# A hybrid recurrent encoder layer on eight cores: conv buffers on page bounds, more staging slots, pauses that take no turn, and an earlier norm of tile 3

## What is computed

```
h = rmsnorm(x, g_mix)
q, k, v, o, if, f_h, i_h, q_h, g_h, gate_a, gate_b = split(h @ w_in)
q, k = silu(causal_conv4(q, k))                    # width 4, per channel
hm, C, n, m = mlstm_chunkwise(q, k, v, i, f)        # matrix memory, 4 heads
y_a = (rmsnorm(hm) * sigmoid(o)) @ w_branch_a
oh, S = hgrn2_chunkwise(q_h, 1 - f, i_h, log f)     # f = lb + (1-lb)*sigmoid(f_h)
y_b = (rmsnorm(oh) * silu(g_h)) @ w_branch_b
x = x + (sigmoid(gate_a)*y_a + sigmoid(gate_b)*y_b) @ w_out
x = x + square(relu(rmsnorm(x, g_ffn) @ w_ff1)) @ w_ff2
y = rmsnorm(x, g_final)
```

## Time and profile before

| | us |
|---|---|
| timed runs: median (lowest, highest) of 3 | 4442.13 (4436.71, 4608.5) |
| profiled execution, its own time | 4419.51 |
| its span, slowest core (cores 4383.6 to 4418.2) | 4418.2 |
| TensorE busy, of the span | 4057.9 |
| ScalarE, VectorE busy | 1386.1, 1387.1 |

### The profile page before, as it was taken

How to read it: one execution, slowest core, us unless ns; L and a number is a source line. 1 busy time by engine, 2 the same in 40 slices (tenths; PEclk the granted TensorE clock), 3 DMA queues, 4 the chain that set the end, 5 groups by cost and what they waited for, 6 DMA issues and landing times.

```text
span 4418.2 us, 60194 instructions; the slowest of 8 cores (4383.6 to 4418.2 us)
## 1 busy us (share of the span) xinstructions
PE 4057.9 (92%) x22402; PEld 1944.4 (44%) x22402; DVE 1387.1 (31%) x2519; ACT 1386.1 (31%) x2730; POOL 272.8 (6%) x517
## 2 busy tenths in 40 slices
PE   6779878889799999997999999998999999999999
PEld 3334334334344444443444444444444445444444
DVE  4325265222333432224233422222542331310012
ACT  4445355221433332104333321124433311122212
POOL 0000000000000000000000000000000000000000
PEclk9989889999899999998999999999999999999999
DMA  9888867888687878986777789876888897677775
GB/s 180 168 178 164 180 136 146 175 165 156 130 173 140 162 137 192 174 168 125 161 148 140 142 176 192 170 148 126 174 155 166 166 196 131 118 125 130 124 125 120
DMA packets 142711, 682.91 MB, mean 155 GB/s; under 512 B 24496, under 2 KB 54712, under 8 KB 69080
## 3 DMA queue, kind: packets, MB, share of 16 engines
q0 software_dynamic: 73872, 536.94, 69.7%
q1 hardware_dynamic: 53344, 111.78, 7.4%
q10 hardware_dynamic: 15208, 30.35, 2.1%
HBM read 1157.17 MB, written 58.74 MB: 275 GB/s over the span
## 4 chain that ended last, share of the span: by engine, by line
PE 78%; DMA 8%; DVE 5%; ACT 5%; issue 3%; ACTq 0%; DVEq 0%; SPq 0%; POOL 0%; POOLq 0%
PE psb L294 76%; DMA wslot<-wu 3%; ACT rr L263 2%; DMA iS<-aa 2%; PE psb L302 1%; DMA kS<-aa 1%; DVE uh L280 1%; DVE rr L272 1%; ACT rq L263 1%; ACT uh L263 1%; DVE rr L280 1%; DVE rr L276 1%; DMA rr<-xp 1%; ACT aa L263 1%; DMA xt<-xp 1%
## 5 line engine op out<-in xcount | busy, mean ns | idle before, releaser
L294 PE MATMUL psb<-ht,wslot 128*128 128x512 bf16 x4096 | 926.7, 388 | 58.4 <-DMA wslot<-wu 24.3
L294 PE MATMUL psb<-wslot,aa 128*128 128x512 bf16 x4096 | 907.2, 381 | 27.9 <-ACT aa L263 26.6
L294 PE MATMUL psb<-uh,wslot 128*128 128x512 bf16 x4096 | 905.7, 380 | 2.6 <-DVE uh L272 1.9
L294 PEld LDWEIGHTS psb<-ht,wslot 128*128 128x128 bf16 x4096 | 405.1, 100 | 559.5 <-issue 107.3
L294 PEld LDWEIGHTS psb<-wslot,aa 128*128 128x128 bf16 x4096 | 396.5, 98 | 503.8 <-issue 46.4
L294 PEld LDWEIGHTS psb<-uh,wslot 128*128 128x128 bf16 x4096 | 396.2, 98 | 471.0 <-issue 12.3
L104 POOL DMA_DIRECT2D wslot<-wu x512 | 272.1, 536 | 4083.6 <-PE psb L294 3897.9
L272 DVE TENSOR_TENSOR xt<-psb,xt 128x512 f32<-128x512 f32 x320 | 221.1, 691 | 956.9 <-PE psb L294 956.7
L263 ACT ACTIVATE rq<-psb 128x512 f32<-128x512 f32 (+1 forms) x320 | 166.9, 521 | 659.0 <-PE psb L294 642.1
L263 ACT ACTIVATE aa<-psb 128x512 f32<-128x512 f32 x160 | 95.3, 595 | 576.8 <-PE psb L294 537.3
L263 ACT ACTIVATE rr<-rr 128x512 f32<-128x512 f32 (+9 forms) x322 | 169.8, 529 | 241.6 <-DVE rr L272 147.5
(11 more groups left out here) (186 smaller groups left out, 2978.6 us busy)
## 6 DMA issues: line engine op xcount, KB each, us to landing
wslot<-wu POOLq DMA_DIRECT2D x512, 1024.0 KB, 13.7
xt<-xp SPq DMA_DIRECT2D x22, 1024.0 KB, 31.1
yp<-xt SPq DMA_DIRECT2D x12, 1024.0 KB, 12.9
ht<-hS SPq DMA_DIRECT2D x5, 2048.0 KB, 12.9
fS<-aa SPq DMA_DIRECT2D x16, 512.0 KB, 15.8
rr<-fS ACTq DMA_DIRECT2D x16, 512.0 KB, 9.4
rr<-xp SPq DMA_DIRECT2D x6, 1024.0 KB, 20.2
vS<-aa SPq DMA_DIRECT2D x8, 512.0 KB, 16.1
```

Of the source, the lines that this page charges most:

```text
L294: ins = pe_e.matmul(out, lhsT=l, rhs=r, start=(i == 0), stop=(i == n - 1))
```

## The change

Five things:

1. **Conv buffers.** The two pads lie at 0 and 2304, three accumulators at 4608 + 2048k, so that none shares a page with another; the conv counter goes through 2 pads, 3 accumulators and 2 `sg` buffers. The put-off `fin` of a unit's last chain, and the store behind it, now run after the next chain's first reads, in the next unit too.
2. **Staging slots.** Tile 0 has eight (4 in `aa`, 4 in `hg`), tile 1 four, tile 2 eight until its unit 9 (4 in `aa`, 4 in `xt`), then four; the fills of t = 0 and 1 have six (2 in `rr`), that of t = 2 four. The sample frames have four of 512 bytes, of which a V or IH result takes two. The gate results take a slot like the others.
3. **Pauses and turns.** A pause yields "w". `pull` then tries the other lane too, and a turn passes only if both pause. In `p12` a chain of K or Q is worth half a pull, any other chain one and a half; elsewhere one, as before. Two pauses are added in `norm_block` between the scaled row and its transposes, and tile 0's recurrence takes the longer form with pauses (`sp`).
4. **Norm of tile 3.** It has two x buffers in `xt`; the first two loads are issued at unit 11 of `p12` of tile 2. A block's next load is issued right after its scaling.
5. **Place of `norm2`'s buffers**: `hg` at 8192 and 12288 for t < 3.

```diff
@@ pull, tick
-                    next(q[0])
-                    bg["last"] = nm_
-                    return True
+                    r = next(q[0])
                 except StopIteration:
                     q.pop(0)
-        return False
+                    continue
+                if r == "w":
+                    waited = True
+                    break
+                bg["last"] = nm_
+                return True
+        return waited
-    def tick():
-        bg["acc"] += bg["rate"]
+    def tick(w=1.0):
+        bg["acc"] += w
@@ norm_block
         yield
+        yield "w"
+        yield "w"
         for half in range(2):
@@ norm1
-            yield from norm_block(xv[0:LB, :], xv.p(), LB, xnviews[b % len(xnviews)], b, PO_GMIX, dst, t0)
+            g = norm_block(xv[0:LB, :], xv.p(), LB, xnviews[b % len(xnviews)], b, PO_GMIX, dst, t0)
+            yield next(g)
+            if b + n < nb:
+                x_load(T, xviews, b + n)
+            yield from g
...
-            if b + n < nb:
-                load(b + n)
-                if n == 1:
-                    for _ in range(5 if blocks is not None else 3):
-                        yield
+            if b + n < nb and n == 1:
+                for _ in range(3):
+                    yield "w"
@@ p12
+        def stage(kind, nb, dt, *shape):
+            stg[kind] += 1
+            if kind == "p":
+                k = stg["p"] % len(slots)
+                return slots[k][0].v(slots[k][1], dt, *shape), f"stp{k}"
...
-                            cv["i"] ^= 1
+                            cv["i"] += 1
                             ns, sl = (1, 512) if p else (2, 32)
-                            o = cvoff + cv["i"] * 4112
-                            pad, acc = cvbuf.v(o, F32, ns, sl + 3), cvbuf.v(o + 2064, F32, ns, sl)
-                            sg = cvbuf.v(cvoff + 8224, F32, ns, sl) if cv["i"] else rq.buf.v(0, F32, ns, sl)
+                            pad, acc = cvbuf.v((cv["i"] % 2) * 2304, F32, ns, sl + 3), cvbuf.v(4608 + (cv["i"] % 3) * 2048, F32, ns, sl)
+                            sg = sg0[0].v(sg0[1], F32, ns, sl) if cv["i"] % 2 else rq.buf.v(0, F32, ns, sl)
...
-                            if late:
-                                late.pop()()
+                                if store is not None:
+                                    store()
+                            flush()
                             late.append(fin)
                         if p:
-                            tick()
-                    if late:
-                        late.pop()()
+                            tick(1.5 if kind == "QH" else 0.5)
@@ build_program, the calls
-    for t in (1, 2):
+    for t in (0, 1, 2):
         tiles[t]["sp"] = True
-    p12([tiles[0]], 0, 12, b_uh, 0, 3, pre0, at0)
+    p12([tiles[0]], 0, 12, b_uh, sg_e, sl(b_aa, 0, 4) + sl(b_hg, 0, 4), pre0, at0)
-    p12([tiles[1]], 0, 12, b_uh, 0, 3)
+    p12([tiles[1]], 0, 12, b_uh, sg_e, sl(b_aa, 0, 4))
-    p12([tiles[2]], 0, 12, b_uh, 0, 3)
+    x3v = [b_xt.v(16384, F32, 2048), b_xt.v(24576, F32, 2048)]
+    at2 = {11: lambda: [x_load(tiles[3], x3v, b) for b in range(2)]}
+    p12([tiles[2]], 0, 12, b_uh, sg_e, sl(b_aa, 0, 4) + sl(b_xt, 16384, 4), None, at2, 9)
...
-                lanes["a"].append(norm1(tiles[3], [b_rr.v(8192, F32, 2048)], [b_rr.v(16384, BF16, 2048)], bl, 8))
+                lanes["n"].append(norm1(tiles[3], x3v, [b_rr.v(16384, BF16, 2048)], bl, 0, True))
...
-            p12([tiles[3], TS_], fill[t][0], fill[t][1], b_rr, 0, 3)
+            p12([tiles[3], TS_], fill[t][0], fill[t][1], b_rr, (b_rr, 10752), sl(b_aa, 0, 4) + (sl(b_rr, 20480, 2) if t < 2 else []))
```

More of the change, by code:

```diff
@@ L428, in norm_block, with x_load, norm1 @@
         yield
-    def norm1(T, xviews, xnviews, blocks=None, gap=4):
+    def x_load(T, xviews, b):
+        LB = T["LB"] if T["kind"] == "p" else 64
+        src = xp[T["id"] * 512:(T["id"] + 1) * 512, :] if T["kind"] == "p" else xs
+        xv = xviews[b % len(xviews)]
+        S.dma("sp", f"xl{b % len(xviews)}", xv[0:LB, :], src[b * LB:(b + 1) * LB, :], (), xv.p())
+    def norm1(T, xviews, xnviews, blocks=None, gap=4, loaded=False):
         LB = T["LB"] if T["kind"] == "p" else 64
         nb = 4 if T["kind"] == "p" else 1
-        src = xp[T["id"] * 512:(T["id"] + 1) * 512, :] if T["kind"] == "p" else xs
         n = len(xviews)
[L436 to L440, removed]
+        if not loaded:
+            for b in range(min(n, nb)):
+                x_load(T, xviews, b)
         for _ in range(gap):
-            yield
+            yield "w"
         for b in range(nb):
@@ L462, in hload, with p12, flush @@
               sum((DR("H", t, b) for b in range(4)), []), T["hT"].p())
-    def p12(ctxs, lo, hi, cvbuf, cvoff, nst, pre=None, at=None):
-        stg = {"i": 0}
+    def p12(ctxs, lo, hi, cvbuf, sg0, slots, pre=None, at=None, cut=None):
+        stg = {"p": 0, "s": 0}
         cv = {"i": 0}
+        late = []
+        def flush():
+            if late:
+                late.pop()()
+        def stage(kind, nb, dt, *shape):
[3 more added lines that the diff above has]
+                return slots[k][0].v(slots[k][1], dt, *shape), f"stp{k}"
+            if nb > 512:
+                stg["s"] += stg["s"] % 2
+                k = stg["s"] % 4
+                stg["s"] += 1
+            else:
+                k = stg["s"] % 4
+            return hgs.buf.v(k * 512, dt, *shape), f"sts{k}"
         for ui, (kind, u) in enumerate(P12U[lo:hi]):
@@ L469, in p12 @@
                 at[ui]()
+            if cut is not None and ui == cut:
+                slots = slots[:4]
             (wt,) = ws_take([UB[kind] + u])
@@ L1064, in build_program @@
     at0 = {3: lambda: lanes["n"].append(norm1(tiles[1], x0v[0:2], [b_uh.v(12288, BF16, 2048)], None, 10))}
-    p12([tiles[0]], 0, 12, b_uh, 0, 3, pre0, at0)
+    sl = lambda b, lo, n: [(b, lo + 4096 * k) for k in range(n)]
+    sg_e = (hgs.buf, 0)
+    p12([tiles[0]], 0, 12, b_uh, sg_e, sl(b_aa, 0, 4) + sl(b_hg, 0, 4), pre0, at0)
     tiles[0]["rh_ok"] = True
@@ L1087, in hook @@
         def hook(i):
-            if i == 2:
+            if i == 2 and t > 0:
                 drain("n")
@@ L1118, in build_program @@
         else:
-            for _ in range(16):
+            while len(lanes["n"]) > 1:
                 pull("n")
```

62 lines of the change are left out of this document (33 added, 29 removed).

## The result

The changed kernel takes 4372.1 us (median of 5 runs) beside 4445.6 for the kernel before in the same session: ratio 0.9834, 95% interval 0.9815 to 0.9853. That is 65 to 82 us, some 74, about half of the 142 forecast, and 1.7%: it lies under the 2% that the prediction asked of "faster", to which it gave 0.68, and in the "same" to which it gave 0.26.

A forecast was written before the change was run, and what follows sets the result against it. TensorE waits for order and single events, idle 230 us in the tiles, `p3` and fills. Terms 35.6 + 8 + 25 + 28 + 35 + 25 - 15 = 142 us take 4419.5 to 4278; with 22.6 for the median, 4300; range 4250 to 4395.

The forecast's parts named there:

- 4.6 was forecast: Conv chain in K and Q units: about 4.6 us with its own pages, in place of 5.40.
- Tile 0: `p12` of tile 0: ScalarE's 37.8 us of slot waits go, 8 of 43.6 idle remain; 35.6 us gained (20 to 43).
- Who is next late is the conv: Tile 0: once slot waits go, the conv limits; four chains fall 4.6 us behind, in place of 7.8.
- Tile 1: Slot and conv gaps go, a 15 us wait for x comes, three recurrence waits of 4 us; 8 gained (-25 to 25).
- the rival of closer steps: V, QH, IH, FH units: recurrence updates some 8 us late at 24 borders; 71 us slower, 4513; chance 0.06.
- Tile 2: No norm runs, slots are free, recurrence ends before the last eight chains; 22 idle left, 25 us gained (5 to 40).
- p3: `p3` of tile 0: the five waits for the scaled x block, 28.3 us, go; 28 us gained (20 to 29).
- The loads are there before the stage: `p3` of tile 0: x loads arrive before it begins, part of the 28 us gain.
- Fills: The three fills: shorter conv chains, put-off product, four sample slots; 38 of 73 idle left, 35 us gained (15 to 55).
- late weights: Same bytes in less time, tile 0 without slack; 15 us lost to late weights (0 to 40).
- Clock: Slow clock after TensorE's gaps costs some 50 us; with half the gaps gone, 25 us gained (10 to 40).
- the second rival: Page bounds and pauses do little; tiles 1, 2 and first two fills keep their waits; 70 us gained, 4372; chance 0.20.

The follow-up runs named there:

- p_pagesl: The changed kernel with turns and pauses as before and tile 3's norm through one x buffer, late; ratio 0.9855 to the kernel before.
- f_x3: The changed kernel with tile 3's first x loads two units earlier and the score tile's x rows in their own buffer; ratio 0.9779 to the kernel before.
- u_turns: The changed kernel with pauses that take a turn and one pull a chain everywhere, as before; ratio 0.9880 to the kernel before.
- u_page: The changed kernel with the conv buffers of before, sharing pages, and two accumulators; ratio 0.9943 to the kernel before.
- u_slots: The changed kernel with three staging slots in aa for every prompt tile; ratio 0.9870 to the kernel before.
- f_gate: The changed kernel with the 16 KB gate store issued from ScalarE's queue in place of SyncE's; ratio 0.9842 to the kernel before.
- g_q1: The changed kernel with gate and second Q unit stores on ScalarE's queue, tile 3's and the score tile's x read early; ratio 0.9819 to the kernel before.

## Why the prediction was half right

**Conv and slots: the mechanism was right.** The copy that waited on a shared page waits no longer; 4.15 us where 4.6 was forecast. The slot waits went. With the turns of before, tile 0 ends at 242.1 (`p_pagesl`), 34.2 us earlier than before, where the term said 35.6; that the two are so near is in part luck, since tiles 1 and 2 give 22.6 of it back.

**Tile 0: 9.1 us in place of 35.6, below the bound of 20.** The step that failed is the choice of who is next late: "Who is next late is the conv". Next late were loads, on the core shown the recurrence's own, asked for right behind their stores: `rr<-gS` stood in ScalarE's program ahead of copies that need nothing of it, and TensorE idled 25.56 us. On the seven other cores it was an x load of tile 1's norm (16.90 us on core 4) and then `rr<-gS`; the medians gain 13.7 us, still under the bound. On every core TensorE idles 18 to 31 us at these places alone, where the term left 8 in all. The row was there: 5.8 us for `gS` in tile 0 before, which I left out beside the 24.6 and 13.2. No run took both waits away, so what they cost together is read from the timelines and not measured.

**Tile 1: -7.6 in place of +8, inside its bounds, with another reason.** ScalarE did not stand waiting for x 33 us into the tile. VectorE stood 15.98 us at 283.84, for a store out of the new slots in `hg` that hm overwrites. The steps of the recurrence waited 4.6 to 11.7 us at six places (264.98, 318.73, 329.75, 383.11, 432.24 and 617.53), not at 24; the rival of closer steps had the mechanism and four times the number. Four of the six lie in tile 1 and sum to 28.4 us, where the sum had 12: with the 9.81 for VectorE in place of the 15 for x, that is most of the difference. (At 329.75 it is the norm's transposes that wait, behind the recurrence's step on VectorE.)

**Tile 2: 35.4 with its clock, forecast 25 and a share of the 25 of clock.** Inside its bounds, and its waits mis-sized: 29 us of idle time are left where 22 were, and 14.20 of them are the slot wait at 546.48, where the term had "the slots are free". It ended at 740, not at about 700, since tiles 0 and 1 did not give what was forecast.

**`p3`: -11.2 in place of +28, out of its bounds.** The step that failed is "The loads are there before the stage". The first two, issued at unit 11, went out at 729.27, 11 us ahead of the stage, and the first square began 30 us into it, after 24.3 us of waiting; the other two blocks' loads went out inside the stage, and the sample frames' at 838.53. Three squares then waited for nothing and the per-block waits of the earlier trace rows are gone, but two remain of 21.46 and 21.70 us, both for loads that SyncE issues behind its stores: the x loads from 729.27 behind two `fS` stores whose median landing is 39.9 us, and `xt<-xs`, 41.07 us in its issue behind stores of `hS`. `f_x3` shows it: with the loads earlier both waits go, and it gives 32 us of the stage (30 in the medians over the cores, 245.6 for 275.3) and 24 of the total back. The turns have a part in it: in `u_turns`, with the loads of the changed kernel, only one of the two waits stands (22.9 us), and the stage takes 254.4.

**Fills: 13.4 + 8.3 + 3.9 = 25.6 with the late weights and clock in them,** where 35 and 15 against it were forecast; idle time fell from 73 to 36 us, as forecast. Late weights are real: from 1041 to 3010 TensorE waits 33.4 us for `wslot`, 19.7 before. They show in the feed-forward stretches, not in the tiles. `f_x3`'s `p3` moves at a DMA share of 1.02 and waits 4.5 us for weights, so the memory did not bind there at 275 us. (The terms shown for the traffic of tile 0, 2 x 29.39 + 17.38, make 76.2 MB and 286 GB/s, not 77 and 290; nothing turns on it.)

**Clock: 25 us were forecast; no run measures it by itself.** It rose in tile 2 (0.89 to 0.95) and the fills, by 0.01 in tiles 0 and 1, and fell in `p3` (0.95 to 0.92), where two gaps of 21 us stand in place of five of at most 10.3.

The 4372 of the second rival is the measured time by luck: it had the conv's period unchanged and `p3` gaining 28, and neither was so. What it says of the page bounds, that they do little, is true of them alone (10 us).

Open are the 48 us that `u_page` gives back, against 10 for the bounds alone. Three slots alone don't hide the gain, since `u_slots` keeps 58 us with them; which of the other parts the bounds need (the put-off product, the third accumulator, the turns), and how much of the 48 falls in the recurrence's steps of tiles 1 and 2, where 23 lie, no run separated.

## What to carry to other kernels

A wait that is removed is worth what lies between it and the next event that holds the same engine, so list for each stage all DMA waits of each in-order engine, the small ones too, before pricing the largest. Put the issue of a load on the engine's queue only where its store has surely landed; sending one store over another queue shortened its wait here from 30.4 to 5.9 us and gained nothing, as the next load's store was as late. Look at all cores before you blame one wait: in tile 0 the slowest core had a 25.6 us gap that seven others did not have, and they lost the same time elsewhere. Test parts alone as well as undone: here 10 us and 48 us were true of nearly the same edit.

## What was not expected of the hardware

In these runs a store's landing time depended on the backlog of the queue it was issued to more than on its size. At nearly the same moment of tile 0 (`f_gate`), 16 KB on ScalarE's queue were landed and their load issued after 7.1 us, while 512 KB that SyncE issued at 174.30 held their load until 207.17, 33 us; the same 512 KB on ScalarE's queue took at most 15.3 (`g_q1`), and 16 KB on SyncE's 31.2 (changed kernel, core 2, 170.65 to 201.83; on core 4, issued at 182.89, at most 11.7). In that stretch (0 to 267) the six x loads into `xt` on SyncE's queue took 38.4 us in the median to land, and q0 took 69% of the DMA engines' time. The Trainium skill (DMA: Bandwidth & Descriptors, Queues, rings and completion order) says that SyncE and ScalarE own one ring each on the same 16 DMA engines and that an engine takes turns between rings packet by packet. By that a transfer shares with other queues and stands behind its own, and these numbers agree.

The Trainium skill (DMA: Bandwidth & Descriptors, Anatomy of one DMA) says that a wait for a semaphore is held on the issuing engine and not in the DMA engine. The 30.38 us above agree: a copy that needed nothing stood behind a load's issue.

The wait also emptied the memory, with a delay. A weight load needs a half slot that TensorE has used up: the last ones went out at 184.03, the next at 225.59. Until 200 the DMA engines still worked on what had been issued; four of the 40 slices of the changed kernel's first 267 us, from 200 to 227, show them at 0.3, 0.2 and twice below 0.1, most of it after TensorE had started again at 208.21:

```profile
DMA  7999799999999999999999999999993200999999
```

So a stretch that looks saturated (0.92 in the mean) still hid a hole of some 20 us that one late issue had made.
